# A streaming encoder step on one core: activations loaded and transposed ahead of their modulation, one early adaLN block summed on VectorE, late sums and the last recurrence placed later

## The reference

```python
mod = (silu(c) @ ada_w + ada_b)                      # (2, 6 * 1024): sh1, sc1, g1, sh2, sc2, g2
h = rmsnorm(x, norm1_w) * (1.0 + sc1) + sh1
z = h @ w_in + b_in
ya, h_last, conv_new = rglru(z[xa], z[ga], ...)      # causal conv, gates, linear recurrence
yb, C, n, m = mlstm(z[q], z[k], z[v], z[o], z[i], z[f], ...)
x = x + g1 * (concat([ya, yb]) @ w_out)
h2 = rmsnorm(x, norm2_w) * (1.0 + sc2) + sh2
x = x + g2 * peer(h2, ...)                           # top-k experts, rows gathered from a table
```

## Time and profile before

| what | value |
|---|---|
| median of 3 runs | 3425.88 us (3415.39 to 3426.16) |
| the profiled execution, its own time | 3421.94 us |
| its span, first to last instruction | 3420.1 us |
| TensorE's granted clock, mean | 0.979 of full |
| PE, DVE, ACT, POOL busy | 86%, 65%, 63%, 36% of the span |
| read from HBM | 1177.76 MB, 347 GB/s over the span |

### The profile page before, as it was taken

How to read it: one execution, slowest core, us unless ns; L and a number is a source line. 1 busy time by engine, 2 the same in 40 slices (tenths; PEclk the granted TensorE clock), 3 DMA queues, 4 the chain that set the end, 5 groups by cost and what they waited for, 6 DMA issues and landing times. The chain is left out here.

```text
span 3420.1 us, 41840 instructions
## 1 busy us (share of the span) xinstructions
PE 2936.9 (86%) x9150; PEld 1403.7 (41%) x9150; DVE 2232.2 (65%) x5470; ACT 2159.1 (63%) x7233; POOL 1216.6 (36%) x1126
## 2 busy tenths in 40 slices
PE   7999999878888888888788888888888888888876
PEld 3555345534433433344344443443343344334331
DVE  3665526567667667666666776666666766676665
ACT  3222114367777777777777776776677777777775
POOL 0000100134444444434444444444344444444443
PEclk9999999999999999999999999999999999999999
DMA  6312121499999999999999999999999999999998
GB/s 241 105 63 79 29 102 64 148 419 412 419 419 411 395 419 418 415 399 419 391 419 404 419 407 417 403 419 378 419 412 419 413 397 420 419 411 394 419 420 337
DMA packets 167939, 1189.87 MB, mean 348 GB/s; under 512 B 19470, under 2 KB 19598, under 8 KB 28282
## 3 DMA queue, kind: packets, MB, share of 16 engines
q0 software_dynamic: 155440, 1118.14, 79.8%
q1 hardware_dynamic: 12236, 68.96, 5.4%
HBM read 1177.76 MB, written 9.25 MB: 347 GB/s over the span
## 5 line engine op out<-in xcount | busy, mean ns | idle before, releaser
L868 PE MATMUL ps<-r_w,r_yT 128*128 128x512 f32 (+1 forms) x3168 | 1520.1, 614 | 336.7 <-ACT r_yT L1169 332.8
L1705 DVE SCALAR_TENSOR_TENSOR r_yT<-r_w,r_qk 128x1024 bf16<-128x1024 f32 x792 | 969.4, 1226 | 690.7 <-DMA r_w<-in_peer_uv,gidx 680.8
L576 POOL DMA_INDIRECT r_w<-in_peer_uv,gidx x792 | 887.0, 1120 | 1008.4 <-PE ps L868 853.2
L868 PEld LDWEIGHTS ps<-r_w,r_yT 128*128 128x128 f32 (+1 forms) x3168 | 550.5, 189 | 1222.9 <-issue 1221.9
L868 PE MATMUL ps<-r_yT 128*128 128x512 f32 (+1 forms) x1056 | 523.5, 630 | 91.6 <-ACT r_yT L1169 80.4
L576 POOL DMA_INDIRECT r_yT<-in_peer_uv,gidx x264 | 291.3, 1103 | 557.3 <-PE ps L868 486.4
L1161 ACT ACTIVATE mixc<-mixc 128x1 f32<-128x1 f32 x1056 | 208.4, 197 | 443.9 <-DVE r_yT L1705 436.0
L1169 ACT ACTIVATE r_yT<-ident,mixc 128x128 f32<-128x128 f32 x1024 | 412.8, 403 | 93.5
L1165 ACT ACTIVATE mixc<-mixc 128x1 f32<-128x1 f32 x1056 | 409.5, 388 | 35.2
L1164 ACT ACTIVATE mixc<-mixc 128x1 f32<-128x1 f32 x1056 | 409.4, 388 | 33.6
L1705 DVE SCALAR_TENSOR_TENSOR r_yT<-r_yT,r_qk 128x1024 bf16<-128x1024 f32 x264 | 322.8, 1225 | 116.1 <-DMA r_yT<-in_peer_uv,gidx 97.6
(11 more groups left out here) (283 smaller groups left out, 2365.4 us busy)
## 6 DMA issues: line engine op xcount, KB each, us to landing
r_w<-in_ada_w SPq DMA_DIRECT2D x16, 1024.0 KB, 5.1
r_w<-in_peer_uv,gidx POOLq DMA_INDIRECT x792
r_w<-in_w_lin SPq DMA_DIRECT2D x16, 512.0 KB, 11.6
r_w<-in_ada_w SPq DMA_DIRECT2D x3, 2048.0 KB, 17.4
r_yT<-in_peer_uv,gidx POOLq DMA_INDIRECT x264
r_vo<-in_x_prompt SPq DMA_DIRECT2D x8, 512.0 KB, 18.5
r_w<-in_w_vo SPq DMA_DIRECT2D x2, 2048.0 KB, 7.8
r_w<-in_w_out SPq DMA_DIRECT2D x2, 2048.0 KB, 8.9
```

The source lines that it names most:

```text
L576: pool.indirect_dma_start(ring[place(h, j)], None, table, bass.IndirectOffsetOnAxis(gidx_t[:, h, j:j + 1], 0))\
L868: mm = nc.tensor.matmul(ps[0:r, 2 * p + c, :], diag[:, j % 4, 0:r], row[:, D + c * 512:D + (c + 1) * 512], start=h == 0 and j == 0, stop=h ...
L1705: V.scalar_tensor_tensor(udump[j % 2], ring[i][:, 0:D], 1.0, h2[:, t, :], ALU.mult, ALU.mult, accum_out=dots[:, i:i + 1]).then_inc(dot_don ...
```

## The change

- SP loads all nine tiles of x first, then adaLN block 0, the two halves of block 3, blocks 1 and 2. `w_lin` blocks 0 to 3 follow without a wait, 4 to 7 wait for the third `ada_mm`. POOL's three small loads (896 KB) wait for the first `ada_mm`.
- Statistics, scaling and turning of x go in groups of three tiles, ahead of the adaLN values. The evictions are plain copies, one instruction of 4x128 columns per tile on DVE and one on ACT.
- Block 3 is done as the late ones are: `ada_part(3)` on DVE, `ada_sum(3)` on PE.
- When `mul1` is there, DVE modulates six of the eight slices of `hT` in place and ACT two (1024 + 32 columns each); PE waits slice by slice, in the first column group only. The nine tiles are no longer mixed with the column groups.
- The small logarithm chain of the recurrence parameters stands at the start of DVE.
- `ada_sum` 5, 7 and 8 stand behind a first column group, 9, 10 and 11 behind a third one; block G3 stands behind q3; `decays(3)` and `roots(3)` follow k0 and k1.

```diff
-            for b in range(4):
-                sp.dma_start(ada[b], A["ada_w"][b].rearrange("p (k n) -> p k n", k=KD)).then_inc(ada_ld[b], 16)
-                if b < 3:
-                    for t in range(3 * b, 3 * b + 3):
-                        sp.dma_start(xin[0:rows(t), t, :], x_rows[t]).then_inc(ld_x[b], 16)
+            for t in range(NT):
+                sp.dma_start(xin[0:rows(t), t, :], x_rows[t]).then_inc(ld_x[t // 3], 16)
...
+            load_block(0)
+            sp.dma_start(abias, bias_rows[0:4].partition_broadcast(2)).then_inc(ld_ab, 16)
+            load_halves(3)
+            load_block(1)
+            load_block(2)
...
+            for t in range(6):
+                turn_x(t)
+            pe.wait_ge(c_silu, 1)
+            ada_block(0)
+            for t in range(6, NT):
+                turn_x(t)
+            ada_block(1)
+            ada_block(2)
+            pe.wait_ge(x_evd, NT)
+            pe.wait_ge(x_eva, NT)
+            ada_sum(3)
...
-            sums = {"xa1": 4, "xa2": 5, "G1": 6, "xa3": 7, "q1": 8, "q2": 9, "q3": 10, "k1": 11}
+            sums = {("xa1", 2): 4, ("q0", 0): 5, ("G1", 2): 6, ("q1", 0): 7, ("ga3", 0): 8, ("q3", 2): 9, ("k0", 2): 10, ("k1", 2): 11}
...
-                    if nblk == 0:
-                        for t in range(3 * g, 3 * g + 3):
-                            turn_x(t)
-                        pe.wait_ge(x_evd, 3 * g + 3)
-                        pe.wait_ge(x_eva, 3 * g + 3)
                     bank = z_bank()
                     for k in range(KD):
+                        if nblk == 0 and g == 0:
+                            pe.wait_ge(h_moda if k % 3 == 2 else h_modd, k // 3 + 1 if k % 3 == 2 else k - k // 3 + 1)
...
+            squares(0)
+            x_root(0)
+            squares(1)
+            x_root(1)
+            evict_x(0)
+            evict_x(1)
+            squares(2)
+            x_root(2)
+            for t in range(2, NT):
+                evict_x(t)
+            act.wait_ge(mul1_ready, 1)
...
+            x_scale(0)
+            x_scale(1)
+            evict_x(0)
+            evict_x(1)
+            x_scale(2)
+            for t in range(2, 6):
                 evict_x(t)
...
+            mod_row(0)
+            for t in range(6, NT):
+                evict_x(t)
+            ada_part(3)
+            for b in range(1, 4):
+                mod_row(b)
...
+            for k in (0, 1, 3, 4, 6, 7):
+                for s, c in ((0, slice(0, SEQ)), (1, slice(SEQ, T))):
+                    m = V.tensor_scalar(hT[:, k, c], hT[:, k, c], mul1[:, s, k:k + 1], modT[:, 0, k, s:s + 1], ALU.mult, ALU.add)
+                m.then_inc(h_modd, 1)
```

More of the change, by code:

```diff
@@ L374, in load_ada @@
             def load_ada(b):
[L375 to L381, removed]
+                load_halves(b)
                 if b >= 6:
@@ L926, in _, with squares @@
-            for t in range(NT):
+            act.wait_ge(lam_abs, 1)
+            nc.scalar.activation(lt1, lt1, ACT.Exp, scale=-1.0).then_inc(lam_exp, 1)
+            nc.scalar.activation(rden[:, 0:1], ones[:, 0:1], ACT.Sqrt)
+            def squares(g):
+                act.wait_ge(ld_x[g], 48)
+                for t in range(3 * g, 3 * g + 3):
+                    r = rows(t)
+                    if t:
+                        act.wait_ge(x_sq, t)
+                    nc.scalar.activation(sq_junk[0:r], xin[0:r, t, :], ACT.Square, accum_out=ssq[0:r, t:t + 1]).then_inc(x_sq, 1)
@@ L927, in _, with x_root, evict_x @@
+            def x_root(g):
+                act.wait_ge(x_var, g + 1)
+                c = slice(3 * g, 3 * g + 3)
+                nc.scalar.activation(ssq[:, c], ssq[:, c], ACT.Sqrt).then_inc(x_rt, 1)
+            def evict_x(t):
                 r = rows(t)
                 act.wait_ge(x_tr, 2 * t + 2)
[L929 to L932, removed]
@@ L1234, in _ @@
[L1234 to L1246, removed]
@@ L1292, in _ @@
-            for t in range(NT):
-                evict_x(t)
             link(V.memset(pick2, 0.0))
@@ new lines, in ada_part @@
+            def ada_part(b):
+                if b >= 4:
+                    dve.wait_ge(ada_mm, b)
+                for k in range(KD):
+                    i = k // 4
+                    if k % 4 == 0:
+                        dve.wait_ge(half_ld[i], 16 * (b - 2))
+                    for s in range(2):
+                        w, c = ada_half[i][:, k % 4, :], csil[:, s, k:k + 1]
+                        if k == 0:
+                            m = V.tensor_scalar(acc[s], w, c, None, ALU.mult)
+                        else:
+                            m = V.scalar_tensor_tensor(acc[s], w, c, acc[s], ALU.mult, ALU.add)
+                        if s == 0:
+                            ch.mark(m)
+                    if k % 4 < 3:
+                        ch.mark(m)
+                        ch.need()
+                    else:
+                        m.then_inc(half_done[i], 1)
+                        dve.wait_ge(half_done[i], b - 2)
+                        ch.need()
```

178 lines of the change are left out of this document (86 added, 92 removed).

## The result

The changed kernel's median is 3396.83 us (3396.73 to 3401.09, 5 runs) beside 3425.88 (3415.39 to 3427.26, 5 runs) before: a ratio of 0.9926, 95% interval 0.9913 to 0.9939. The profiled execution took 3396.78 us, 25.2 less than that of before, where the sum said 20.4. Two more sessions gave the kernel before medians of 3419.95 and 3420.80, and a third, with the same changed kernel again, 3422.70 against 3396.45 (ratio 0.9929, 0.9915 to 0.9942): 26 us.

A forecast was written before the change was run, and what follows sets the result against it. PE was taken to bound up to the experts, table fetches after. Gains of 7.0 (start) and 13.4 (late part) sum to 20.4 us, giving 3401.5 from 3421.94 or 3405.5 from the median; forecast 3402.5, range 3391 to 3413 us.

The forecast's parts named there:

- Two stages in a row, only the front counts: Whole kernel: PE paces up to the experts, table fetches after; time won in the front moves the rest as a block.
- The start: PE's own program becomes the bound, first z matmul at 57, first block 16.2 us, its end 7.0 us earlier: Up to the first z block's end: first matmul 3.6 us later, block 10.6 us less, end from 80.2 to 73.2.
- The ends of the range: First z block's end: 8.6 or 5.4 us earlier, for a first z matmul at 55.6 or 58.7, instead of 7.0.
- rival 5: Start and late part both better: full-clock transposes, no give-back, 24.5 us plus the gates' clock, 3394 to 3398 us; chance 0.15.
- PE stays at 1.2 GHz through the start: Start: slow adaLN blocks add 19 to 21 us; 13 lost, 13.4 won late, 3422 to 3426 us; chance 0.05.
- The transfers land in time: Start: last needed adaLN block near 38.9; z blocks 0 to 3 before 50, 4 to 7 covered until needed at 116.
- The terms that I put at nothing: Start: POOL's loads, 2 us of rate nobody waits for; z blocks 4 to 7 covered; DVE's block 3 part hidden.
- The copies at nothing: Start: nine copies, 6.2 us of DVE, hidden under adaLN blocks 0 and 1; rival had them on the path, chance 0.05.
- The late part: 15.9 removed, 2.5 given back, 13.4: Late adaLN sums: 12.3 us of waits and 3.6 of slow sums removed, new waits 2.5; net 13.4, 10 to 17.
- Slower, by a chain held back on DVE: Late part: later sums push the recurrences by 48 us, more than 20 reaching PE, 3420 to 3453 us; chance 0.02.
- The total: Whole kernel: 7.0 at the start plus 13.4 late, 20.4 us less; forecast 3402.5 us.

The follow-up runs named there:

- e4: Changed kernel with block 3 as 8 matmuls on PE instead of DVE's sum with PE's 2 matmuls; median 3401.38 us, 0.9941 of the kernel before.
- e5: Changed kernel with evictions of tiles 0, 1 and 2 ahead of the next group's scales and squares; median 3398.32 us, 0.9938 of the kernel before.
- e7: Changed kernel with the order of e5 plus 44 unread matmuls before the first tile (the run between had only these, 3400.18 us); median 3401.35 us.
- e8: Changed kernel with tiles turned as before, scale and shift in the evictions; load order and block 3 on DVE stay; median 3405.59 us, ratio 0.996.
- e1: Kernel before with only the late part (moved sums, G3, decays(3), roots(3)); median 3404.02 us against 3419.95, ratio 0.995.
- e3: Changed kernel with sums 9 and 10, G3, decays(3) and roots(3) at their old places; median 3401.10 us, 0.994 of the kernel before.

## Why the prediction was right, point by point

- **Two stages in a row, only the front counts.** Right, by the table: the rest is 2750.4 to 2754.3 in all fourteen profiles.
- **The start: PE's own program becomes the bound, first z matmul at 57, first block 16.2 us, its end 7.0 us earlier.** Right in numbers: 56.82, 16.4, 7.25, some of it by luck. The first tile was on PE at 13.60 and not at 12.5, tile 2 at 19.36 and not at 18.6, tile 4 at 24.77 and not at 24: each about 1 us late. Block 0 began at 27.97, past the upper end of my 26 to 27.7. What evened it out is that block 0 ran at full clock behind transposes at the lower one, where I had put both on the same clock. The headline is half wrong: PE bounds only from block 0 on (e4), and ahead of it the scaled tiles do (e5 to e7). The steps under the headline had these waits in them. The ends of the range should read 8.4 and 5.3, not 8.6 and 5.4 (80.2 less 71.8 and less 74.9), which moves rival 5 by 0.2.
- **PE stays at 1.2 GHz through the start.** Did not happen: all three adaLN blocks took 7.03. The rival's text gives the waits before the second to fourth blocks of before as 1.7; the one before the second was 2.96.
- **The transfers land in time.** Right; block 2 even somewhat earlier than 38.9 (by 37.3 in e8). The terms that I put at nothing (POOL's loads, z blocks 4 to 7, the part of block 3) did not reach PE: the sum of block 3 started with no wait at 51.18, and from 60 us on PE has no wait for a transfer.
- **The copies at nothing.** Right for those from block 0 on: PE has no wait between 27.97 and the bias rows. Not shown for the first ones: ACT's copies of tiles 0 and 1 stand ahead of its third group of squares, which begin at 17.77, while the root of the group before had ended at 16.3; and e5, with one more copy there, had the scales behind them 1.2 us later. No run prices the copies by themselves.
- **The late part: 15.9 removed, 2.5 given back, 13.4.** Mechanism right, size low: 15.3 (e1, and 278.1 to 262.9 in the changed kernel). Given back were 1.9, at sums 6 and 11 as said; but sum 11's part was held back by the later decays of the last recurrence and not by sum 10:

```profile
278.44 1.26 DVE L1402 SCALAR_TENSOR_TENSOR r_yT<-r_yT,r_vo 128x1059 f32<-128x1059 f32 x1 [6.38 <-ACT r_vo L1020]
```

Sum 10 had ended at 275.8 by then. The other piece is the gate matmuls behind slow sums, which I named but left out of the sum. Before, behind sum 8 and behind sum 9, they read:

```profile
223.57 2.50 PE L647 MATMUL ps<-r_vo,r_wr 128*128 128x353 f32 x6
...
263.69 2.92 PE L647 MATMUL ps<-r_vo,r_wr 128*128 128x353 f32 x6
```

and in the changed kernel:

```profile
203.75 1.95 PE L662 MATMUL ps<-r_vo,r_wr 128*128 128x353 f32 x6
...
254.92 2.05 PE L662 MATMUL ps<-r_vo,r_wr 128*128 128x353 f32 x6
```

That is 0.55 + 0.87 = 1.4 us. 12.3 + 3.6 + 1.4 - 1.9 = 15.4.
- **Slower, by a chain held back on DVE.** Did not happen. DVE did wait 5.40 us, for which the profile names no releaser; sum 9 ended at 255.0, just before:

```profile
255.09 0.68 DVE L1312 TENSOR_TENSOR r_wq<-ps,r_wq 2x512 f32<-2x512 f32 x1 [5.40 <-issue]
```

Of what follows on DVE only sum 11's accumulators reached PE late, by the 1.06 us above.

- **The total.** 20.4 forecast; 22.5 of front in the first profile. The term that was mis-sized is the late part, by 2. The measured 3396.83 is 5.7 under the 3402.5 that I forecast and lies in the range of rival 5, though rival 5's reasons did not hold: two waits were given back, and the transposes ahead of block 0 were slow. That it lies inside my range owes something to the width of the range. The medians' 29.0 in the first session contains the spread of the kernel before, whose 38 times lie between 3415.39 and 3427.26 with a median of 3421.9. Against that, the change is 25 us. In the first profile 2.7 us of that lie behind the first fetch, and no run here separates them from chance. In the repeat only 0.3 do: of its 26.0 us (3420.1 to 3394.1), 23.9 are the front and 1.7 the group of 48 matmuls behind it at the higher clock.

## What to carry to other kernels

Where an engine waits for several things in a row, the last due time counts, and not the sum of its idle rows. Two ways to shorten a wait or speed up PE ahead of that time, and both together, won nothing, since the idle time moved to the next wait; moving a loaded block of work into the gap won 5.1 us at the first z matmul. A consumer that works in program order can ask for a late product one step later: here moving the place of the asking was enough, and 12.3 us of waits became 1.9. A second pass over the data cost less here than it won, since it let the transposes start early and most of the first pass lay under other engines' work. And pieces of a change may be worth nothing one by one: turning ahead without block 3 on DVE won 1.4 us at the end of the first block (80.45 to 79.06), block 3 on DVE without turning ahead nothing (80.59), both 7.3.

## What the runs showed of the hardware that I had not expected

The same order of instructions gets the clock at different places from run to run. PE's sixteen transposes at 19.4 took 2.40 us in the changed kernel and 1.94 in its repeat; the granted clock at 20 to 22 us was

```profile
20.00:22.00 2.00, 1.76 (x12) 0.68 1.00 414
```

in the first, and

```profile
20.00:22.00 2.00, 1.38 (x13) 1.00 0.98 397
```

in the second. The first z block took 14.7 to 17.5 us over the kernels with the new start; in the shortest, the repeat of the changed kernel, the granted clock was 1.00 all along, and in the longest, e3, it was 0.50 from 57 to 62 us. A difference of 2 us in a front of 336 can therefore be the draw of the clock, and only repeats tell such edits apart.
